# A mixed-attention block on one core: V products ahead of the input's deviation, query units next, cache rows stored a stage later, projections one step later

## The reference

```python
def reference(...):
    h = rms_norm(x, norm_mix_g)
    q_a, kv_a, gate_a, qkv_b, u_c, v_c, gate_m = split(h @ w_in)
    o_a = gate_branches(sigmoid(gate_a), o_cmp, o_sel, o_win)   # compressed, selected, window attention
    o_b = dilated attention of qkv_b                            # later stages
    o_c, v_rows = sgu_mixer(u_c, v_c, ln_g, ln_b, w_s, b_s)
    x = x + m @ w_out ; x = x + relu(rms_norm(x) @ w_up)^2 @ w_down

def sgu_mixer(u, v, ln_g, ln_b, w_s, b_s):
    u = gelu(u)
    v = layer_norm(gelu(v), ln_g, ln_b)
    w_c = tril(w_s)                                 # per head, 128 x 128
    mixed = einsum('hts,bcshd->bcthd', w_c, v_chunks) + b_s
    return u * mixed, v

def compressed(q, rows, cmp_pe, cmp_w1, cmp_b1, cmp_w2):
    blocks of 32 rows at stride 16, + cmp_pe; gelu(blocks @ cmp_w1 + cmp_b1) @ cmp_w2   # keys and values
```

## Time and profile before

| what | value |
|---|---|
| median of the runs | 1860.03 us (1859.1 to 1861.97) |
| the profiled execution, its own time | 1859.93 us |
| its span | 1858.3 us |
| its mean granted PE clock | 0.962 |
| PE busy | 1740.5 us |
| DVE, ACT, POOL busy | 663.4, 330.7, 176.1 us |
| stage one | to 202.43 us |
| stage two | to 564.69 us |

### The profile page before, as it was taken

One profiled execution on the slowest core, in us unless ns is written; L12 is line 12 of the kernel. 1 busy time (PEld: TensorE's weight loads), 2 busy tenths in 40 slices (PEclk: granted clock), 3 DMA queues, 4 the chain that ended last, 5 costly groups with the idle time before them and its releaser, 6 DMA issues. The chain is left out here.

```text
span 1858.3 us, 27096 instructions
## 1 busy us (share of the span) xinstructions
PE 1740.5 (94%) x10458; PEld 1377.8 (74%) x10458; DVE 663.4 (36%) x1565; ACT 330.7 (18%) x841; POOL 176.1 (9%) x312
## 2 busy tenths in 40 slices
PE   6999999999989999999996888888998999999997
PEld 3687788889977777777773545556887888888885
DVE  3431243443340232323223122101466666543234
ACT  2310033333330122222230121210001000000000
POOL 0000000000000000100004576460000000000000
PEclk8999799999998999999997999899999999999999
DMA  8999333333337998621306999896522222222221
GB/s 309 328 344 338 105 112 92 92 92 92 114 114 244 355 310 299 215 83 56 103 27 234 354 341 325 295 306 245 179 68 68 83 77 91 71 88 91 68 91 49
DMA packets 150922, 322.78 MB, mean 174 GB/s; under 512 B 19397, under 2 KB 88328, under 8 KB 149770
## 3 DMA queue, kind: packets, MB, share of 16 engines
q1 hardware_dynamic: 119626, 178.58, 29.7%
q0 software_dynamic: 26560, 129.62, 20.4%
q10 hardware_dynamic: 4608, 12.85, 1.9%
HBM read 303.57 MB, written 109.25 MB: 222 GB/s over the span
## 5 line engine op out<-in xcount | busy, mean ns | idle before, releaser
L1357 PE MATMUL bank<-hT,wring 128*128 128x272 f32 x1408 | 346.0, 396 | 0.6 <-PEq L1155 0.6
L1357 PEld LDWEIGHTS bank<-hT,wring 128*128 128x128 f32 x1408 | 259.9, 191 | 58.1 <-issue 10.3
L895 PE MATMUL bank<-wring,w 128*128 128x128 f32 x2048 | 246.1, 277 | 1.1 <-DVE hidp L815 1.1
L895 PEld LDWEIGHTS bank<-wring,w 128*128 128x128 f32 x2048 | 235.8, 192 | 11.2 <-issue 10.7
L1790 POOL DMA_DIRECT2D ring<-in_sel_pages x256 | 141.5, 553 | 315.1 <-issue 260.0
L2175 PEld LDWEIGHTS bank<-hT,xk 128*128 128x128 f32 x512 | 99.5, 200 | 50.4 <-issue 28.9
L2175 PE MATMUL bank<-hT,xk 128*128 128x272 f32 x512 | 133.1, 415 | 0.0
L2428 PE MATMUL bank<-hT,wring 128*128 128x272 f32 x392 | 95.4, 392 | 0.0
L2428 PE MATMUL bank<-aT,wring 128*128 128x272 f32 x352 | 85.9, 392 | 0.0
L2428 PEld LDWEIGHTS bank<-hT,wring 128*128 128x128 f32 x392 | 74.5, 190 | 15.4
L317 POOL DMA_DIRECT2D out_new_dil<-in_cache_dil x24 | 15.3, 641 | 739.2 <-POOLq L1155 408.5
(11 more groups left out here) (357 smaller groups left out, 2311.3 us busy)
## 6 DMA issues: line engine op xcount, KB each, us to landing
wring<-in_w SPq DMA_DIRECT2D x147, 512.0 KB, 4.5
out_new_dil<-in_cache_dil POOLq DMA_DIRECT2D x8, 8176.0 KB, 35.1
wring<-in_cmp_pages SPq DMA_DIRECT2D x256, 128.0 KB, 2.2
ring<-in_sel_pages POOLq DMA_DIRECT2D x256, 64.0 KB, 4.7
ring<-in_sel_pages SPq DMA_DIRECT2D x256, 64.0 KB, 4.4
out_new_dil<-in_cache_dil POOLq DMA_DIRECT2D x8, 2032.0 KB, 13.0
ring<-in_dil_k SPq DMA_DIRECT2D x9, 1024.0 KB, 10.0
ring<-in_dil_k POOLq DMA_DIRECT2D x9, 1024.0 KB, 7.6
```

What stands on the lines that cost most here:

```text
L895: last = pe.matmul(banks[6 + c % 2][:, P * part:P * part + P].rearrange("p (g a s) -> p g a s", g=G, s=8), w1[:, kv, 8 * hf + jj, :], x[:, ...
L1357: mm = pe.matmul(banks[6 + hf][:, 0:HT], ring_slot(wr, u)[:, k * P:k * P + P], hT[:, k, HT * hf:HT * hf + HT], start=(k == 0), stop=(k == ...
```

## The change

1. The deviation is applied behind the V products. DVE first multiplies the input by the norm's weights in place (`s_xg`); PE multiplies that by the V units, and the rows are scaled by 1/deviation per row when DVE reads the bank. For that PE turns the deviations into a column (`s_rr`, `rcol`). PE's order is: products of slice 0 for all five row groups, sums of squares 0 to 3, products of slice 1, squares 4 to 7, slices 2 and 3, then row group by row group slices 4 to 7, the sample rows first. Each group has a bank of its own. Units 0 and 1 are issued between the input's slices. `hT` is written for the T tiles alone.
2. The weight units stand in the order V, query, U, keys and values, gates. The query tiles are copied out between the V rows' GELU steps.
3. The bias of the mixing is added by DVE (`mixed`), from a tile that is loaded by two broadcasts; the bias products are gone. The four groups have banks of their own, the sample parts share bank 3 and are combined once. New rows and gates are transposed before group 3; the sample gates are transposed too (`gate_s`).
4. SP stores the gate rows in two DMAs and the new rows in one. The gate rows' return and the 16 stores of window rows are issued by POOL in stage two; `newn` lives on into it.
5. A request's projection moves from the end of the even pair to the odd pair behind it, before its flips; the last one stands at the end of pair 15.

```diff
-U_U = U_V + 4
-U_A = U_U + 4
-U_DIL = U_A + 11
+U_Q = U_V + 4
+U_U = U_Q + 4
+U_KV = U_U + 4
+U_DIL = U_KV + 7
...
+        ROWS = (NI,) + tuple(range(NI))
...
+        def v_product(pe, i, k):
+            m = rows_of(i)
+            return pe.matmul(v_bank(i)[0:m, :], xT[:, k, i * P:i * P + m],
+                             ring_slot(wr, U_V + k // 2)[:, (k % 2) * 512:(k % 2) * 512 + 512],
+                             start=(k == 0), stop=(k == KD - 1))
...
+        def mix_bank(n):
+            return banks[(1, 4, 5, 0)[n]]
...
+                    if k in (0, 3):
+                        load_units(sp, wr, k // 3, 1)
+                load_units(sp, wr, 2, RING - 2)
...
+                for hh in range(2):
+                    sp.dma_start(bs[hh * DH:hh * DH + DH, :, :],
+                                 t["bs"][hh:hh + 1].to_broadcast([DH, 4, P + NS])).then_inc(s_sgl, 16)
...
-                sp.wait_ge(s_gate, 1)
-                for i in range(24):
-                    g, r, c = i // 12, i // 3 % 4, i % 3
-                    sp.dma_start(t["scr_gate"][:, g, :, r:r + 1, c].rearrange("b s o -> o b s"),
-                                 gate_t[i:i + 1, SEQ:NT].rearrange("o (b s) -> o b s", s=S),
-                                 allow_slow_non_contiguous=True).then_inc(s_scr, 16)
...
-                sp.dma_start(t["scr_v"], newn[:, 0:2, :]).then_inc(s_scr, 16)
-                for i in range(2):
-                    for b in range(B):
-                        sp.dma_start(t["new_win"][b, 512 - S:512, P * i:P * i + P],
-                                     newn[S * b:S * b + S, 2 + i, :]).then_inc(sm["store_done"], 16)
-                sp.wait_ge(s_scr, 16 * 25)
-                sp.dma_start(bgate[:, :, :], t["scr_gate"].rearrange(
-                    "(t j) g s r c -> (j g s r) t c", t=2)).then_inc(s_rows, 16)
...
+                sp.wait_ge(s_tr_read, 4)
+                for g in range(G):
+                    sp.dma_start(t["scr_gate"][:, g].rearrange("b s r c -> b s (r c)"),
+                                 gate_s[:, 12 * g:12 * g + 12]).then_inc(s_scr, 16)
+                sp.dma_start(t["scr_v"], newn[:, 0:2, :]).then_inc(s_scr, 16)
...
+                def a_half(n):
+                    act.wait_ge(sm["w_used"], n + 5)
+                    dst = qaT[:, n, :] if n < 4 else kvT[:, n - 8, :]
+                    act.activation(dst[:, 0:HT], banks[n % 2][:, 0:HT], ACT.Copy).then_inc(s_t_read, 1)
...
+                for i, at in enumerate(ROWS):
+                    m = rows_of(at)
+                    act.wait_ge(s_vz_read, i + 1)
...
+                    act.activation(tmp[0:m, 0:512], vn[0:m, at, :], ACT.Square).then_inc(s_gel0, 1)
...
+                    if i >= 2:
+                        a_half(i - 2)
+                a_half(3)
...
                 for k in range(KD):
-                    dve.wait_ge(x_landed[k], 16)
-                last = dve.memset(var[:, :], 1.0)
-                ch.count(last)
-                rms_dve(dve, ch, xT, hT, 0, rstd)
+                    dve.wait_ge(sm["sq_ready"], k + 1)
+                    dve.tensor_scalar(xT[:, k, :], xT[:, k, :], norm_g[:, 0, k:k + 1], None,
+                                      ALU.mult).then_inc(s_xg, 1)
+                dve.wait_ge(sm["std_ready"], 1)
+                dve.reciprocal(rstd[:, :], rstd[:, :]).then_inc(s_stat, 1)
+                dve.wait_ge(s_stat, 1)
+                dve.wait_ge(s_xg, KD)
+                def normed(k):
+                    dve.tensor_tensor(hT[:, k, :], xT[:, k, :], rstd[:, :], ALU.mult).then_inc(
+                        sm["h_ready"], 1)
+                for k in range(4):
+                    normed(k)
+                dve.wait_ge(s_rr, 1)
+                turned = banks[2][:, 0:32 * NI + 32].rearrange("p (i c) -> p i c", c=32)
+                ch.count(dve.tensor_copy(rcol[:, 0:NI], turned[:, 0:NI, 0]))
+                ch.link(dve.tensor_copy(rcol[0:NS, NI:NI + 1], turned[0:NS, NI, 0:1]))
...
+                for i, at in enumerate(ROWS):
+                    m = rows_of(at)
+                    v = vn[0:m, at, :]
+                    dve.wait_ge(s_vz, i + 1)
+                    dve.tensor_scalar(v, v_bank(at)[0:m, :], rcol[0:m, at:at + 1], None,
+                                      ALU.mult).then_inc(s_vz_read, 1)
+                    if i == 0:
+                        for k in range(4, KD):
+                            normed(k)
...
+                    if i >= 2:
+                        a_tile(i - 2)
+                a_tile(3)
...
+                def mixed(n):
+                    x = (tmp, tmp2)[n % 2][:, 0:512]
+                    dve.wait_ge(s_mix, n + 1)
+                    ch.link(dve.tensor_tensor(
+                        x.rearrange("p (c q) -> p c q", c=NI),
+                        mix_bank(n)[:, :].rearrange("p (c q) -> p c q", c=NI),
+                        bs[:, n, 0:P].unsqueeze(1).to_broadcast([P, NI, P]), ALU.add))
+                    ch.count(dve.scalar_tensor_tensor(out=ocT[:, n, 0:SEQ], in0=x, scalar=0.5,
+                                                      in1=uT[:, n, 0:SEQ], op0=ALU.mult, op1=ALU.mult))
+                for n in range(3):
+                    mixed(n)
...
+                dve.tensor_copy(gate_s[:, :], banks[7][0:NS, NI * 24:NI * 24 + 24]
+                                ).then_inc(s_tr_read, 1)
+                mixed(3)
+                ch.wait()
+                x = tmp[:, 0:4 * NS].rearrange("p (n q) -> p n q", n=4)
+                ch.link(dve.tensor_tensor(x, banks[3][:, 0:4 * NS].rearrange("p (n q) -> p n q", n=4),
+                                          bs[:, :, P:P + NS], ALU.add))
+                ch.link(dve.scalar_tensor_tensor(out=ocT[:, :, SEQ:NT], in0=x, scalar=0.5,
+                                                 in1=uT[:, :, SEQ:NT], op0=ALU.mult, op1=ALU.mult))
...
-                rms_pe(pe, sq, 0)
+                for k in range(4):
+                    if k % 2 == 0:
+                        unit_landed(pe, U_V + k // 2)
+                    pe.wait_ge(s_xg, k + 1)
+                    for i in ROWS:
+                        last = v_product(pe, i, k)
+                    if k % 2:
+                        last.then_inc(sm["w_used"], 1)
+                    if k < 2:
+                        for j in range(4 * k, 4 * k + 4):
+                            squares_pe(pe, j)
+                pe.wait_ge(s_xg, KD)
+                for i in ROWS:
+                    for k in range(4, KD):
+                        if i == ROWS[0] and k % 2 == 0:
+                            unit_landed(pe, U_V + k // 2)
+                        last = v_product(pe, i, k)
+                        if i == ROWS[-1] and k == 5:
+                            last.then_inc(sm["w_used"], 1)
+                    last.then_inc(s_vz, 1)
+                    if i == ROWS[0]:
+                        pe.wait_ge(s_stat, 1)
+                        for j in range(NI + 1):
+                            m = rows_of(j)
+                            last = pe.transpose(banks[2][0:m, 32 * j:32 * j + 32],
+                                                rstd[0:32, j * P:j * P + m], ident[0:32, 0:32])
+                        last.then_inc(s_rr, 1)
+                pe.wait_ge(s_vz, NI + 1)
+                pe.sem_inc(sm["w_used"], 1)
                 pe.wait_ge(sm["h_ready"], KD)
...
+                pe.wait_ge(s_vz_read, 1)
...
-                        pe.matmul(dst, half[:, :], bb, start=True, stop=False)
...
+                            r = slice(hh * DH, hh * DH + DH)
+                            dst = mix_bank(n)[r, c * P:c * P + P] if c < NI \
+                                else banks[3][r, n * NS:n * NS + NS]
                             w = wsT[:, h, :] if c < NI else ws4[:, h, :]
-                            last = pe.matmul(dst[hh * DH:hh * DH + DH, :],
-                                             vn[0:m, c, h * DH:h * DH + DH], w, start=False,
+                            last = pe.matmul(dst, vn[0:m, c, h * DH:h * DH + DH], w, start=True,
                                              stop=True)
                     last.then_inc(s_mix, 1)
...
+        def projects(n, last):
+            return n % 2 == 1 and (n == len(PAIRS) - 1) == last
         def group2_at(n, kind, k=0):
-            return FIRST_GROUP2[n] + {"flip": k, "sum": PAIRS[n][1] + 2, "project": PAIRS[n][1] + 3}[kind]
+            if kind == "project":
+                return FIRST_GROUP2[n + 1] - 1 if projects(n, True) else FIRST_GROUP2[n]
+            return FIRST_GROUP2[n] + projects(n, False) + {"flip": k, "sum": PAIRS[n][1] + 2}[kind]
...
+                pool.wait_ge(s_scr, 48)
+                pool.dma_start(bgate[:, :, :], t["scr_gate"].rearrange(
+                    "(t j) g s r c -> (j g s r) t c", t=2)).then_inc(s_rows, 16)
+                for i in range(2):
+                    for b in range(B):
+                        pool.dma_start(t["new_win"][b, 512 - S:512, P * i:P * i + P],
```

(52 more changed lines are left out.)

135 lines of the change are left out of this document (48 added, 87 removed).

## The result

The kernel before took 1861.0 us (median of 4, 1859.1 to 1864.02), the changed one 1835.52 (median of 4, 1832.61 to 1845.35; two more executions on record took 1839.04 and 1848.99): ratio 0.9883, 95% interval 0.9841 to 0.9925. Measured again later, beside the experiments, it was 1827.64 (median of 6) against 1864.94, ratio 0.9802, interval 0.978 to 0.9825. It is faster both times, by 1.2% and by 2.0%; the forecast was 2.6% (1811 us), with a range that ends at 1828: the first measurement lies outside it, the second at its edge. The profiled execution took 1845.35 us, some 10 more than the median.

What follows compares the result with a forecast made beforehand. TensorE, busy 94% of the span, was taken as the bound. Terms 12.8 + 16.5 + 10.4 + 6.2 + 3.2 = 49.1 us off the profiled 1859.93 gave 1811 us, range 1802 to 1828.

Steps and rivals of the forecast that it cites:

- Start: Beginning of stage one: V products start at 6.7 us, before the deviation is known, T tiles at 51.9 for 64.66: -12.8 us.
- The slow beginning: First V products of stage one: 2.3 us added for TensorE starting at the lower clock.
- Tail: From the T tiles to stage two's first scores: bias products gone, 27.5 us becomes 11, -16.5 us.
- the chain: End of stage one: VectorE's operations behind the T tiles sum to 9.85 us and bound the tail at 10.4.
- rival E: Start of stage two: first pages late beside the bulk copies, costing 1 to 6 us, 1817 us; chance 0.06.
- Stage two: Request projections moved later: four inner waits for hidden rows vanish, -10.4 us, and the lost clock returns, -6.2 us.
- rival B: Stage two: the wait only moves, TensorE waits for scores or flips in odd pairs, 1827 us; chance 0.12.
- The last projection: End of stage two: pair 15's flips and sums run ahead of it, inside 6.76 us of idle TensorE: -3.2 us.
- the prediction's last sign: Stage two: the prediction is wrong where TensorE waits for VectorE in the odd pairs; no size given.
- rival D: Tail of stage one: the clock falls at the first transposes, tail 18.7 us, 1819 us; chance 0.06.
- Rival C: Start of stage one: interleaved inputs and weights come too late, half of 12.8 us gained, 1817 us; chance 0.10.
- Rival F: Stage one: mixed products keep TensorE at the lower clock through V products and T tiles, up to about 1960 us; chance 0.02.

Runs made afterwards that it cites:

- experiment 1: Changed kernel, but GpSimd issues four bulk cache copies in stage one and the fifth in stage two behind its 17 small transfers: 1831.32 us (0.9823).
- experiment 2: Changed kernel, but ScalarE's queue issues the fifth bulk copy, behind its last operation of stage one: 1829.29 us (0.9797).
- experiment 5: Changed kernel with four bulk copies in stage one and the other 28 in stage three, none beside stage two: 1820.59 us (0.9749).
- experiment 8: Changed kernel run again, unchanged: 1827.64 us.
- experiment 3: Kernel before, with four bulk copies in stage one and the fifth issued by GpSimd at the start of stage two: 1885.64 us (1.0101).
- experiment 6: Kernel before, with four bulk copies in stage one and 28 in stage three: 1867.2 us (0.9999).
- experiment 9: Changed kernel with four bulk copies in stage one, 28 in stage three, and six thrown-away TensorE products behind stage one's last mixing product: 1816.63 us (0.9765).
- experiment 10: Changed kernel with four bulk copies in stage one, 28 in stage three, and twelve thrown-away TensorE products ending stage one: 1823.28 us (0.9791).
- experiment 12: Changed kernel with four bulk copies in stage one, 28 in stage three, and three thrown-away TensorE products ending stage one: 1813.28 us (0.9717).
- experiment 7: Changed kernel with all 32 bulk copies in stage three, none in stage one: 1824.24 us (0.9799).

## Why the prediction was wrong

*Start*, -12.8 forecast, -11.8 measured. Right, by its own steps: first product at 6.7 as said, T tiles at 52.89 for 51.9. VectorE's work hid, and the T tiles kept their price. The slow beginning, 2.3 forecast, is there: the first ten records of V products take 6.86 us, the next ten 4.68. That it is the lower clock, as the prediction has it, the rows do not say: the granted clock reads 1.00 from 6 to 12 in both kernels.

*Tail*, -16.5 forecast, -0.8 measured. **This is the step that failed.** Its two halves must be kept apart. The work was forecast well: VectorE bounds it, 9.56 us where the chain gave 9.85; four mixing records took 1.09/4 = 0.27 us, near the 0.25 of L1064 and far from 0.44; SyncE ended with VectorE. What failed is the list of those who must be done before the stage ends. It held TensorE, VectorE and SyncE. GpSimd was in it only for the stores newly given to it, and the bulk copies only in rival E, as traffic beside the first pages. The rows that tell of them were in reach: issue at 155.81 before, landing at 191.9. Stage two was to start at about 173. A stage that gives up 29 us of cover must be compared with everything that ended under this cover. With that step stage two starts at 191.9 + 0.5 = 192.4 and not at 51.9 + 110.3 + 11 = 173.2, and the forecast is 1811 + 19.2, some 1830. (In the changed kernel the copy took 31.9 us, and stage two started at 189.83.) Experiments 1, 2, 5 and 8 show the cause, 3 and 6 that the copy cost nothing before.

*Stage two*, -10.4 and -6.2 forecast, -16.8 measured for both together. Right: the four inner waits are gone, and up to pair 14 no new one is over 0.6 us, so rival B falls. The last projection, -3.2 forecast, -1.4 measured, is where the one large wait of stage two now stands, 4.8 us, in an odd pair and for VectorE, as the prediction's last sign has it. The text had the flips and sums of pair 15 inside the 6.76 us of idle TensorE. The flips need VectorE's scaled scores (`att`), which came late in both kernels; the rows are VectorE's before and TensorE's in the changed kernel:
```profile
554.83 0.47 DVE L1149 TENSOR_SCALAR att<-att,att_d 128x128 f32<-128x128 f32 x2
...
534.34 1.11 PE L1080 MATMUL bank<-con,att 128*128 128x128 f32 x4 [4.78 <-DVE att L1210]
```
Before, `att` was ready at 555.30 and `hid` at 557.29: only 2.0 of the 6.76 us could be filled, and TensorE still idles for 4.78. Then the sums wait for ScalarE's flip copies and run from 536.50 to 538.17, when `hid` is ready at 536.27. Moving the projection in front of them would only exchange two pieces of TensorE work, and was not tried.

*What no step had*: the start of stage two at the lower clock, +8.4 us. The forecast asked whether the clock falls in the tail (rival D), and it did not: 1.00 from 160 to 170, through eight transposes and the mixing. "TensorE: Matmul & The Clock Gate", section "Part 4: PE-mode transpose", of the Trainium skill says that a transpose does not count as TensorE being busy in the same way; the 1.1 us of them here did not lower the clock. It fell in the idle time behind, which the change makes deep where there had been work at the lower clock up to 200, and came back behind the eight scores, 3.78 us, before, after 23 us in the profile of the changed kernel. Why it takes so long in one run and not in another stays open. That the idle gap brings it on is shown by experiments 9, 10 and 12, where it is closed and all three profiles run at 7.33 us, against two of seven without (two of five where the gap is 3.05 us), and by the clocks of the executions under experiment 12.

*Rival C* (inputs late) fell: 6.70. *Rival E* was right in mechanism where the fifth copy was moved beside the pages, but its price, 1 to 6 us, was far too low: 7.3, 15.5 and 21.7 us. In the changed kernel it does not occur, since the stage's end waits until the copy has landed. The rule of the Trainium skill that I set beside it ("DMA: Bandwidth & Descriptors", section "SWDGE vs HWDGE vs iDMA") I had read as equal shares. The queues' rows of experiment 3 show 8.37 MB against 2.01; the same section says that an engine changes over at packet boundaries, and if its packets are those that the profile counts, of 7.1 and 0.8 KB here, that would favour the copy, as it did. *Rival F* fell.

The difference from the forecast is then about 16 us at the stage's end, up to 8 of clock in five of the seven profiles, and 2 at the end of stage two, 26 in all, give or take what runs differ by in stage four. With the first two taken away again (experiment 12) the kernel takes 1813.28 us, 2 over the forecast; with single executions from 1803 to 1817, that it comes so near is partly luck.

## What to carry to other kernels

When a change shortens the tail of a stage, make a list of everything that was still in flight under the old tail, with its landing time: every queue, GpSimd's software transfers above all, which here hold the end of a stage until they have landed. Whatever lands after the new end of the work is the new bound. Move such a transfer to a stage that needs no memory at its start, not just over the boundary: the 8 MB copy cost 17 us where it held the end, 7 to 22 where it ran beside the first pages, and nothing inside a stage bound by TensorE. And an idle gap of 3 us between two stages can cost 8 more at the lower clock; 2.8 us of products with no purpose brought stage three some 10 us sooner in the profiles, and the median is 7.5 us lower, measured on another chip and with overlapping intervals.

## What the runs showed of the hardware

- Stage two started only when the transfer that GpSimd had issued in stage one had landed (188.99 and 189.83 for landings at 188.5 and 189.3), while one of the same size on ScalarE's queue was in flight for 22 us more without holding the start.
- Of two streams that ran at once (experiment 3, 200 to 235), the one with 7.1 KB a packet got 70.8% of the DMA engines' time and the one with 0.8 KB 19.8%.
- The clock stayed at 1.00 through transposes and 64-column mixing, and was at 0.50 from 172 on, TensorE having been idle since 170.2. The scores and small products at the head of stage two brought it back after 4 us in the kernel before (0.92 in 206 to 208), after 5 in experiment 7 and after 23 in the changed kernel.
- Stage four, bound by its transfers, differs by up to 18 us (276.5 to 294.1) between executions of the same code: a difference of a few us of the whole kernel is to be read from the stage, not from the total.
